# A decoder layer on one core: the relative-bias rows made by one product after the projection, tile stores issued between loads, and another order of weight sums and activation stores

## What is computed

```
x = x + 0.5 * swiglu(rms_norm(x), w_gu, w_down)          # ffn1, 2816 wide
h = rms_norm(x) @ w_in                                   # q, k, v and pool channels
a = sliding_window_attention(q, k, v, rel_bias, sinks)   # scores + rel_bias[bucket(q - k)]
m = multiscale_pool(u)
x = x + concat(a, m) @ w_out
x = x + 0.5 * swiglu(rms_norm(x), w_gu2, w_down2)        # ffn2
gate = sigmoid(rms_norm(x) @ ple_w_gate + b)
e = rms_norm(p @ ple_w_proj)                             # needs p alone, not x
out = x + gate * e
```

## Time and profile before

| | |
|---|---|
| Time, median of 3 runs | 1750.92 us (1748.47 to 1754.02) |
| Time of the profiled execution | 1750.57 us |
| Its span (first to last instruction) | 1748.7 us |
| TensorE busy | 1699.0 us, 97% of the span |
| VectorE, ScalarE, GpSimd busy | 72%, 40%, 13% |
| Mean granted TensorE clock | 0.988 of full speed |

### The profile page before, as it was taken

The page is one execution under the profiler, slowest core; times in us unless marked ns, Lnnn a source line. Parts: engine busy times, 40 slices in busy tenths (PEclk is TensorE's granted clock), DMA queues, the critical chain, the costliest instruction groups (busy, mean ns, idle before and its releaser), DMA issues.

```text
span 1748.7 us, 20495 instructions
## 1 busy us (share of the span) xinstructions
PE 1699.0 (97%) x7362; PEld 1380.9 (79%) x7362; DVE 1251.1 (72%) x1803; ACT 701.7 (40%) x1128; POOL 230.9 (13%) x245
## 2 busy tenths in 40 slices
PE   7989999999989999999999999999999999999998
PEld 5878888888878888776677788888888887888877
DVE  5988777777546768687877788776667664676785
ACT  5633332333335444456655443232232234534442
POOL 0012111112110000044130001212121120000000
PEclk9999999999999999999999999999999999999999
DMA  8235545454479765121123214553444358876433
GB/s 302 78 109 205 187 173 195 176 179 156 152 258 319 217 193 167 60 65 58 45 68 119 83 62 146 185 183 143 178 147 152 138 174 295 277 244 195 161 110 121
DMA packets 127024, 282.94 MB, mean 162 GB/s; under 512 B 10539, under 2 KB 52172, under 8 KB 118348
## 3 DMA queue, kind: packets, MB, share of 16 engines
q1 hardware_dynamic: 123616, 275.55, 46.7%
q10 hardware_dynamic: 3308, 6.08, 0.9%
HBM read 202.95 MB, written 78.64 MB: 161 GB/s over the span
## 4 chain that ended last, share of the span: by engine, by line
PE 74%; DVE 13%; DMA 5%; ACT 4%; issue 2%; POOL 2%; SPq 1%; ACTq 0%; DVEq 0%; POOLq 0%
PE bank L833 24%; PE bank L834 24%; PE bank L835 24%; DMA wdr<-in_wd 2%; POOL wdr L815 2%; DVE qb L1879 1%; DVE hn L1500 1%; PE bank L1082 1%; DMA d_f<-in_wd 1%; ACT probs L1424 1%; DVE w_lo L1708 1%; DVE probs L1891 1%; DVE dn_lo L1700 1%; ACT dn_hi L1233 1%; DVE h_lo L1506 1%
## 5 line engine op out<-in xcount | busy, mean ns | idle before, releaser
L1700 DVE TENSOR_TENSOR dn_lo<-d_f,dn_hi 128x1024 fp32r<-128x1024 f32 x154 | 191.6, 1262 | 125.3 <-ACT dn_hi L1233 124.6
L815 POOL TENSOR_TENSOR wdr<-wdr 128x256 f32<-128x256 f32 x176 | 165.8, 942 | 840.0 <-DMA wdr<-in_wd 829.7
L833 PE MATMUL bank<-h_hi,t_hi 128*128 128x512 f32 x704 | 274.7, 390 | 0.0
L835 PE MATMUL bank<-h_hi,t_lo 128*128 128x512 f32 x704 | 273.9, 389 | 0.0
L834 PE MATMUL bank<-h_lo,t_hi 128*128 128x512 f32 x704 | 273.9, 389 | 0.0
L833 PE MATMUL bank<-dn_hi 128*128 128x512 f32 x616 | 243.3, 395 | 9.7 <-DVE dn_lo L1700 9.7
L834 PE MATMUL bank<-dn_lo,dn_hi 128*128 128x512 f32 x616 | 241.6, 392 | 0.0
L835 PE MATMUL bank<-dn_hi,dn_lo 128*128 128x512 f32 x616 | 241.4, 392 | 0.0
L1233 ACT ACTIVATE dn_hi<-d_f 128x1024 fp32r<-128x1024 f32 x154 | 160.5, 1056 | 166.4 <-DMA d_f<-in_wd 92.7
L833 PE MATMUL bank<-c_hi,t_hi 128*128 128x512 f32 x544 | 212.8, 391 | 5.0 <-DVE t_lo L1555 5.0
L834 PE MATMUL bank<-c_lo,t_hi 128*128 128x512 f32 x544 | 212.5, 391 | 0.0
(11 more groups left out here) (165 smaller groups left out, 2498.3 us busy)
## 6 DMA issues: line engine op xcount, KB each, us to landing
raw<-in_gu SPq DMA_DIRECT2D x44, 1024.0 KB, 5.8
actc<-acts SPq DMA_DIRECT2D x22, 1792.0 KB, 7.0
d_f<-actc SPq DMA_DIRECT2D x154, 256.0 KB, 3.5
raw_m<-in_units SPq DMA_DIRECT2D x52, 512.0 KB, 4.1
wdr<-in_wd SPq DMA_DIRECT2D x44, 512.0 KB, 6.4
wdc<-wdr SPq DMA_DIRECT2D x44, 512.0 KB, 3.4
d_f<-wdc SPq DMA_DIRECT2D x88, 256.0 KB, 3.4
d_f<-in_wd SPq DMA_DIRECT2D x66, 256.0 KB, 4.7
```

The source lines that it names most:

```text
L815: pool.tensor_tensor(blocks[to], blocks[one], blocks[two], ALU.add).then_inc(wd_made, 1)
L833: pe.matmul(ps, whi, vhi, start=first, stop=False, skip_group_check=onto)
L835: return pe.matmul(ps, wlo, vhi, start=False, stop=last, skip_group_check=onto)
L1700: dve.tensor_tensor(dn_lo[slot][:, :], d_f[slot][:, :], plain(dn_hi[slot][:, :]), ALU.subtract).then_inc(dn_split, 1)
```

## The change

**Bias rows.** One product with the 8 columns of `rel_bias` as weights gives an 8 x 384 tile, behind the 16 projection tiles. ACT copies it once (behind the tile copies), SP stores the 8 rows (`band_row`), and in SP's turn of quad 4 one transfer from HBM to HBM repeats each row 128 times into `band`. ACT's and DVE's waits for `band_out` in the first quads go or become a wait for `band_row_out`.

**Start.** The other loads of x and of quad 1 are issued behind tile stores 3, 7 and 11. ACT squares four tiles ahead of the first tile copy; `norm_sum(0)` stands behind the third projection tile instead of the fifth.

**Quad 2.** DVE makes the first `lo` part of quad 3 first and does `mix_acts(ph, 0)` behind `make_c22(2)` instead of ahead of the quad.

**Down weights.** Chunks begin in SP's turn of quad 2, load and store together (`wd_chunk`), with two chunks in the turns 6, 10, 14 and 17, so that turn 19 has the last.

**Last activations.** The eleventh `act_store` becomes four stores (`LAST`), each ahead of one ring load of steps 7 to 10, each with a semaphore of its own.

```diff
+LAST = [(0, 1), (1, 3), (3, 5), (5, 7)]
 WDC_AT = {Q5: 0, Q7: 1, Q4: 2, Q6: 3}
 N_WD = 2 * FH
+
+WD_TWO = (6, 10, 14, 17)
+WD_TURN, _at = {}, 0
+for _q in range(2, QUADS):
+    _n = min(2 if _q in WD_TWO else 1, N_WD - _at)
+    WD_TURN[_q] = tuple(range(_at, _at + _n))
+    _at += _n
...
+BAND_QUAD = 4
...
-        gband_at = [cb + 24 * KB + 4 * SKEW * h for h in range(5)] + hn_at + [extra_at]
-        gband = [place(f"gband{h}", (P, SKEW), gband_at[h]) for h in range(N_Q_HEADS)]
+
+        gband = place("gband", (N_Q_HEADS, SKEW), cb + 24 * KB)
         oh_sb = place("oh_sb", (N_BUCKETS + 1, SKEW), t_at(t_slot(FIRST + 2)))
-        relb = place("relb", (N_BUCKETS + 1, N_Q_HEADS, P), t_at(t_slot(FIRST + 2)) + 4 * SKEW)
...
+            def last_store(ph, i):
+
+                lo, hi = LAST[i]
+                sp.wait_ge(act_mixed, 4 * (ph + 1) * FH)
+                sp.dma_start(actc[ph, FH - 1][:, lo:hi, :], acts[:, lo:hi, :]).then_inc(last_out[i], 16)
+
+            def wd_chunk(ph, c):
+                wd_load(ph, c)
+                wd_store(ph, c)
...
+                if k == FH - 1:
+                    piece = [j for j, (lo, hi) in enumerate(LAST) if lo <= s < hi][0]
+                    sp.wait_ge(last_out[piece], 16 * (ph + 1))
+                elif s == P1:
+                    sp.wait_ge(act_out, 16 * (ph * (FH - 1) + k + 1))
+                if s in WDC_AT:
                     sp.wait_ge(wd_out, 16 * (ph + 1) * N_WD)
...
                         act_store(ph, q // 2 - 1)
-                    wd_load(ph, q - 1)
+                    if ph == 0 and q == BAND_QUAD:
+
+                        sp.wait_ge(band_row_out, 16)
+                        sp.dma_start(band, band_row.unsqueeze(1).to_broadcast([N_Q_HEADS, P, SKEW])).then_inc(band_out, 16)
+                    for c in WD_TURN.get(q, ()):
+                        wd_chunk(ph, c)
                     if q == QUADS - 1:
                         ring_load(ph, 4)
...
-                wd_load(ph, N_WD - 1)
                 ring_load(ph, 5)
-                wd_store(ph, N_WD - 1)
                 for i in range(RING, STEPS):
-                    if i == RING + 1:
-                        act_store(ph, FH - 1)
+                    if RING + 1 <= i <= RING + len(LAST):
+                        last_store(ph, i - RING - 1)
                     if i == FH + 1:
                         sp.wait_ge(wd_out, 16 * (ph + 1) * N_WD)
-                        sp.wait_ge(act_out, 16 * (ph + 1) * FH)
+                        for j in range(len(LAST)):
+                            sp.wait_ge(last_out[j], 16 * (ph + 1))
                         sp.wait_ge(act_made, (ph + 1) * 2 * QUADS)
...
-            sp.dma_start(rel_sb[0:N_BUCKETS, :], rel).then_inc(rel_in, 16)
             p_load(0)
             sp.dma_start(pj_raw[1][:, :], units[W_PROJ + 1]).then_inc(pj_in[1], 16)
             x_load(1)
             p_load(1)
+            sp.dma_start(rel_sb[0:N_BUCKETS, :], rel).then_inc(rel_in, 16)
             quad_load(0, 0)
-            x_load(2)
-            x_load(3)
-            quad_load(0, 1)
-            for h in range(N_Q_HEADS):
-                sp.wait_ge(band_copied, h + 1)
-                sp.dma_start(band[h], gband[h][:, :]).then_inc(band_out, 16)
             for n in range(2 * KT):
                 sp.wait_ge(e_copied, n + 1)
                 sp.dma_start(e_dram[n // KT, :, n % KT, :], et[n % 4][:, :]).then_inc(e_out[n % 4], 16)
+                if n in (3, 11):
+                    x_load(2 + n // KT)
+                elif n == 7:
+                    quad_load(0, 1)
+            sp.wait_ge(band_copied, 1)
+            sp.dma_start(band_row, gband[:, :]).then_inc(band_row_out, 16)
...
-            pe.wait_ge(oh_in, 16)
-            for h in range(N_Q_HEADS):
-                pe.wait_ge(rel_spread, h + 1)
-                if h >= len(band_bank):
-                    pe.wait_ge(band_copied, h - len(band_bank) + 1)
-                pe.matmul(band_bank[h % len(band_bank)][:, 0:SKEW], relb[:, h, :], oh_sb[:, :], start=True, stop=True).then_inc(band_made, 1)
...
-                    if n == 4:
+                    if n == 2:
                         pe.wait_ge(const_in, 16)
                         norm_sum(0)
+            pe.wait_ge(oh_in, 16)
+            pe.wait_ge(rel_in, 16)
+            pe.wait_ge(rel_one, 1)
+            pe.matmul(band_bank[0:N_Q_HEADS, 0:SKEW], rel_sb[:, :], oh_sb[:, :], start=True, stop=True).then_inc(band_made, 1)
             ffn(0)
...
-                if ph == 0 and q == 1 and a == 0:
-                    act.wait_ge(band_out, 16 * N_Q_HEADS)
...
-            for h in range(4):
-                band_copy(h)
             round_pj(0)
             round_pj(1)
-            for h in range(4, N_Q_HEADS):
-                band_copy(h)
             act.wait_ge(small_in, 16)
+            for k in range(KH):
+                x_square(0, k)
             for n in range(2 * KT):
                 e_tile(n)
-                if n < 4:
-                    x_square(0, 2 * n)
-                    x_square(0, 2 * n + 1)
-                elif n == 4:
+                if n < 2:
+                    x_square(0, KH + 2 * n)
+                    x_square(0, KH + 2 * n + 1)
+                elif n == 2:
                     std(0)
-                elif n in (5, 6):
-                    round_first(0, n - 5)
-                elif n >= 8:
-                    round_s(0, "h", 0, n - 8)
+                elif n in (3, 4):
+                    round_first(0, n - 3)
+                elif n >= 6 and n - 6 < KT:
+                    round_s(0, "h", 0, n - 6)
+                elif n >= 6 + KT:
+                    round_first(0, n - 6 - KT + 2)
+            act.wait_ge(band_made, 1)
+            act.activation(gband[:, :], band_bank[0:N_Q_HEADS, 0:SKEW], ACT.Copy).then_inc(band_copied, 1)
             for k in range(KT):
-                if k < FIRST - 2:
-                    round_first(0, k + 2)
+                if k < FIRST - 4:
+                    round_first(0, k + 4)
                 x_square(1, k)
...
-                mix_acts(ph, 0)
...
+                if q == 2:
+
+                    split_t(ph, *todo[0])
                 if more:
                     add_t(ph, q + 1, 0)
                     add_t(ph, q + 1, 1)
@@ -1678,11 +1703,14 @@
                 if more:
                     add_t(ph, q + 1, 2)
                     add_t(ph, q + 1, 3)
+                if more and q > 2:
                     split_t(ph, *todo[0])
                 make_w3(ph, q)
                 for x in todo[1:3]:
                     split_t(ph, *x)
                 make_c22(ph, q)
+                if q == 2:
+                    mix_acts(ph, 0)
...
-            dve.memset(relb[:, :, :], 1.0).then_inc(rel_one, 1)
-            dve.wait_ge(rel_one, 2)
-            dve.wait_ge(rel_in, 16)
-            for h in range(N_Q_HEADS):
-                dve.tensor_scalar(relb[:, h, :], relb[:, h, :], rel_sb[:, h:h + 1], None, ALU.mult).then_inc(rel_spread, 1)
...```

SP at the start. The names are `p_raw` and `x_sb` for the inputs, `et` for the projection tiles, `raw` for the quads. Before:

```order
L721 DMA p_raw<-in_pT 128x2x512
L598 DMA raw_84<-in_gu 128x2048
L725 DMA x_sb<-in_xT 128x4x512 x2
L598 DMA raw_85<-in_gu 128x2048
L739 DMA band<-gband_185 128x384 [waits band_copied]
```

36 lines of the change are left out of this document (17 added, 19 removed).

## The result

The changed kernel takes **1742.16 us** (median of nine runs, 1737.11 to 1745.14) against 1750.43 for the kernel before in the same comparison (nine runs, 1748.47 to 1754.02): ratio 0.9943, 95% interval 0.9928 to 0.9959. That is 8.3 us less. The forecast was 1725.0, range 1719 to 1737: the kernel gained a third of what was forecast.

What follows compares the result with a forecast made beforehand. TensorE was busy 97% of the span, so time could come only from its waits and lower-clock stretches. Start 5.9, quad 2 5.8 and down starts 14.0 sum to 25.7 us, taking 1750.57 to 1724.9 us; range 1719 to 1737.

Steps and rivals of the forecast that it cites:

- The broadcast in quad 4: 1.5 MB transfer in SP's queue in quad 4: about 6 us, costing nothing to the chunk load, POOL and quad load behind.
- The doubled turns: Two chunks in one SP turn: 12.6 us instead of 8.6, costing nothing if quads come in time; cover 6 us.
- The rival "Slower": Turns with two chunks starve VectorE of quads; at 5 us per turn and more, 1765 us; chance 0.03.
- The start: Projection up to the first ffn product: that product starts at 41.5 us against 47.35, gain 5.9 us.
- this case: At the kernel's start, landings later than 14.2 us or a late tile store: gain 2 instead of 5.9, 1729 us; chance 0.11.
- Quad 2: TensorE's wait for `make_c22` in quad 2 falls from 5.0 to 1.3 us; gain 5.8 us, bounds 3.7 and 5.8.
- the rule of the shared pair: VectorE with two SBUF inputs and GpSimd reading SBUF block each other; in full, the chunk's additions add 4.45 us.
- the first rival: In quad 3, VectorE's chain becomes the wait again: 3 us of wait and 2 of clock, 1730 us; chance 0.16.
- its second mechanism: Before quad 3, the store of pair 0 lands as late as at present, when VectorE waits 5.06 us for it.
- The down starts: Start of both down products: losses of 7.9 and 6.1 us go whole, 14.0 us together; bounds 10 and 14.0.
- The sum: Whole kernel: 5.9 + 5.8 + 14.0 = 25.7 us gained, a time of 1724.9 us.

Runs made afterwards that it cites:

- the second trace: The changed kernel run once more, unaltered but for a constant that nothing reads; median 1741.25 us, the traced execution 1744.95 us.
- single_ffn1: Changed kernel with one weight chunk a turn in the first ffn, the last behind the sixth ring load; second ffn keeps doubled turns: 1734.33 us.
- band_18: Changed kernel with the broadcast of the bias rows issued in turn 18 instead of turn 4, nothing else: 1728.21 us.
- two_from_10: Changed kernel, broadcast still in turn 4, second chunks in turns 10, 14 and 17 and the twentieth chunk in turn 18: 1728.21 us.
- down_mix: Kernel before with the new chunk schedule, the last store in four pieces and quad 2's late differences; old start and bias products stay: 1728.57 us.

## Why the prediction was wrong, point by point

- **The broadcast in quad 4** is the step that failed: "Behind it wait the chunk load, POOL and `quad_load(7)`, which isn't used for more than a quad (19.0 us, 84 matmuls): nothing." The delay of that turn was sized rightly (6.9 us against about 6). I asked only who waits in that turn, and named the quad load, which has a quad of cover. The queue's later entries don't: VectorE waits 38.6 us for activation stores and ScalarE 39.6 for `e_part` loads, against 5.3 and 1.7 with the broadcast in turn 18. In place of nothing the price is 14 us in the median (1742.16 - 1728.21).
- **The doubled turns**: "The following odd turn starts late and ends late by about as much as SP idles in it, so the next activation store leaves on time." True from an SP that is on time: 1728.21 both with the broadcast behind all of them and with the first double in turn 10. Untrue for turn 6 behind turn 4. Each was costed from an undisturbed queue, and the two delays were never added. The rival "Slower" (0.03) had late doubled turns, but by the chunks alone, and it had VectorE starved of quads; VectorE waited for stores, and never for `raw`.
- **The start**, 5.9 us forecast: 5.05 in the first trace (47.35 less 42.30), 1.9 in the second (45.41), about 1.5 between the median traces of the new start and the old (45.4 and 46.9), 0.4 in the medians of the times. The third tile came as forecast (16.63 against 17.3). The term that failed is "stores now stand ahead of the later loads, and each has four tiles, 5.4 us": the ninth store stands directly behind the second quad load, stores took up to 6.7 us (8.1 in the second trace), and ScalarE waited 2.5 and 3.9 us. I had named this case and its price (2 in place of 5.9) and given it 0.11.
- **Quad 2**, 5.8 us forecast: the wait fell from 5.0 to 1.4, without a fall of the clock. Undoing only the differences costs 4.7 us, adding only them gives 5.0. Right. With the first chunk's additions back beside the nine instructions (single_ffn1) the wait there is 1.95 us, 0.5 more than 1.4; the rule of the shared pair (the Trainium skill, "SBUF — State Buffer", section "Who interferes with whom") in its full form would have made it 4.45 more, and the run doesn't show that. In that run quad 3 waits 2.3 us for `make_c22`, which is the first rival by its second mechanism: VectorE waits 7.6 us for the store of pair 0 ahead of it. In the changed kernel that wait is 3.1 us, the chunk's additions (4.6 us) lie in quad 3 as well, and quad 3, which had 1 to 2 us of cover, doesn't wait.
- **The down starts**, 14.0 us forecast, 15.2 with the additions of quad 2: 17.0 measured alone on the kernel before. Right in mechanism, a little small. The four pieces were unneeded beside the rest: without the last chunk even a whole store of 1.8 MB is covered.
- **The sum**: with 17.0 and 5.0 from the runs and nothing from the start, 1750.5 - 22.0 = 1728.5, which is what band_18, two_from_10 and down_mix each measure (1728.2 to 1728.6). The remaining 14 us of 1742.2 are the broadcast with the doubled turn 6.

The cause is shown by undoing either member of that pair. The growth of the lateness up to turn 6 is seen in both kernels with the broadcast in turn 4, and is harmless until the second chunk follows. Why SP, once that late, doesn't catch up in the single turns 7 to 9 and 11 to 13 stays open; longer landings don't explain it, as two_from_10 has them too. Eight turns with an eighth of the broadcast each cost as much as one with all of it; the pieces stood in both doubled turns, 6 and 10, and no run separates that from their bytes.

## What to carry to other kernels

Cost a transfer in a shared queue by every later entry of that queue, up to the first turn in which the queue idles, and not by the entries that stand next to it; then add all delays that fall between two such idle stretches. A delay that is covered alone may not be covered as the second. Where a large transfer has no early reader, put it into the turn that has the least behind it.

At a start where TensorE has several short pauses, a term of the sum can come out with or without a loss of clock. The sum should carry a range for it, and the comparison of medians settles it, not one trace.
